# Attention: prompt pairs from slot 0 of the first period, blocks in the order 2, 3, 0, 1

## What is computed

```python
def fox_prompt_attention(q, k, v, cum, valid):   # 4 blocks of 128 queries, 16 heads of 64
    s = jnp.einsum('bqhd,bkhd->bhqk', qi, k).astype(jnp.float32) * FOX_SCALE
    s = s + jnp.swapaxes(ci, 1, 2)[..., :, None] - cum_k[:, :, None, :]
    p = jax.nn.softmax(jnp.where(mask, s, MASK_VALUE), axis=-1)
    return jnp.einsum('bhqk,bkhd->bqhd', p.astype(v.dtype), v)
...
k_past = cache_k[page_table].reshape(DB, P, FOX_HEADS, FOX_DH)
v_past = cache_v[page_table].reshape(DB, P, FOX_HEADS, FOX_DH)
o = fox_sample_attention(q, k_past, v_past, cum_past, k_new, v_new, cum_new)
```

## Time and profile before

| | us |
|---|---|
| median of 3 runs | 2024.12 |
| lowest, highest | 2014.05, 2030.99 |
| the profiled execution | 2018.67 |
| its span, first to last instruction | 2016.5 |
| PE busy in the span | 1935.1 |
| DVE, ACT, POOL busy | 1040.9, 691.8, 440.3 |
| mean granted clock | 0.984 |

### The profile page before, as it was taken

How to read it: one execution, slowest core, us unless ns; L and a number is a source line. 1 busy time by engine, 2 the same in 40 slices (tenths; PEclk the granted TensorE clock), 3 DMA queues, 4 the chain that set the end, 5 groups by cost and what they waited for, 6 DMA issues and landing times.

```text
span 2016.5 us, 35645 instructions
## 1 busy us (share of the span) xinstructions
PE 1935.1 (96%) x14855; PEld 1779.8 (88%) x14855; DVE 1040.9 (52%) x1170; ACT 691.8 (34%) x898; POOL 440.3 (22%) x106
## 2 busy tenths in 40 slices
PE   6999999999899999999999999799998999999998
PEld 6979969979789999999999999655555999999998
DVE  4445245245446865455532535567664566646461
ACT  4131232232224325152531432244444332515251
POOL 2302402412303312121133233000001332121212
PEclk9999999999999999999999999899998999999999
DMA  5351441441243223222232221789996222222231
GB/s 162 126 165 45 137 164 46 137 157 52 95 167 95 84 68 101 82 85 83 98 94 64 65 84 44 215 233 279 280 277 222 85 84 78 90 84 96 71 104 47
DMA packets 197349, 239.13 MB, mean 119 GB/s; under 512 B 16419, under 2 KB 168355, under 8 KB 197027
## 3 DMA queue, kind: packets, MB, share of 16 engines
q1 hardware_dynamic: 175650, 183.27, 30.1%
q10 hardware_dynamic: 21488, 53.46, 8.1%
q0 software_dynamic: 80, 0.52, 0.1%
HBM read 210.77 MB, written 26.12 MB: 117 GB/s over the span
## 4 chain that ended last, share of the span: by engine, by line
PE 68%; issue 16%; DVE 6%; POOL 4%; ACT 2%; DMA 2%; SPq 1%; ACTq 1%; DVEq 0%; POOLq 0%
PE PS L800 12%; PE PS L801 11%; PE PS L802 11%; POOL w_lo L740 4%; PE PS L816 4%; PE PS L818 4%; PE PS L817 4%; PE PS L879 3%; PE PS L880 3%; PE PS L881 3%; PE PS L1349 2%; PE PS L1304 1%; PE PS L1250 1%; PE PS L1284 1%; DVE k_page_t L2366 1%
## 5 line engine op out<-in xcount | busy, mean ns | idle before, releaser
L740 POOL TENSOR_TENSOR w_lo<-w_raw,w_hi 128x2048 fp32r<-128x2048 f32 (+2 forms) x101 | 439.1, 4348 | 1543.5 <-ACT w_hi L1453 1543.5
L1453 ACT ACTIVATE w_hi<-w_raw 128x2048 fp32r<-128x2048 f32 (+2 forms) x101 | 178.1, 1764 | 644.4 <-PE PS L802 419.1
L800 PE MATMUL PS<-hidden_hi,w_hi 128*128 128x296 f32 (+1 forms) x1024 | 304.4, 297 | 0.7 <-DVE hidden_tmp L2135 0.6
L802 PE MATMUL PS<-hidden_hi,w_lo 128*128 128x296 f32 (+1 forms) x1024 | 304.7, 298 | 0.0
L801 PE MATMUL PS<-hidden_lo,w_hi 128*128 128x296 f32 (+1 forms) x1024 | 304.2, 297 | 0.0
L800 PE MATMUL PS<-x_hi,w_hi 128*128 128x296 f32 (+1 forms) x896 | 269.4, 301 | 5.4 <-DVE x_lo L1898 2.8
L801 PE MATMUL PS<-x_lo,w_hi 128*128 128x296 f32 (+1 forms) x896 | 268.4, 300 | 0.0
L802 PE MATMUL PS<-x_hi,w_lo 128*128 128x296 f32 (+1 forms) x896 | 267.8, 299 | 0.0
L879 PE MATMUL PS<-w_hi,x_hi 128*128 128x256 f32 x800 | 225.8, 282 | 0.4 <-DVE fox_gate L2287 0.4
L881 PE MATMUL PS<-w_lo,x_hi 128*128 128x256 f32 x800 | 224.8, 281 | 0.0
L880 PE MATMUL PS<-w_hi,x_lo 128*128 128x256 f32 x800 | 224.6, 281 | 0.0
(11 more groups left out here) (294 smaller groups left out, 3869.4 us busy)
## 6 DMA issues: line engine op xcount, KB each, us to landing
w_raw<-in_w_mlp_up SPq DMA_DIRECT2D x32, 1024.0 KB, 5.4
w_raw<-in_w_mlp_down SPq DMA_DIRECT2D x32, 1024.0 KB, 5.1
k_page<-in_cache_k SPq DMA_DIRECT2D x256, 128.0 KB, 5.7
v_page<-in_cache_v ACTq DMA_DIRECT2D x56, 512.0 KB, 8.0
w_raw<-in_w_ret_in SPq DMA_DIRECT2D x24, 1024.0 KB, 5.4
sample_state<-in_state_ret SPq DMA_DIRECT2D x32, 512.0 KB, 5.3
out_state_ret_sample<-sample_state ACTq DMA_DIRECT2D x32, 512.0 KB, 4.3
w_raw<-in_w_ret_out SPq DMA_DIRECT2D x16, 512.0 KB, 3.5
```

Of the source, the lines that this page charges most:

```text
L740: pool.tensor_tensor(lo, raw, hi.bitcast(F32), ALU.subtract).then_inc(lo_done, 1)
L800: pe.matmul(o, wh[:, w], xh[:, t, cols], start=(t == 0), stop=False)
L802: last = pe.matmul(o, wl[:, w], xh[:, t, cols], start=False, stop=(t == kt - 1))
L1453: act.activation(part(WH[n.slot], n, kt), part(WR[n.slot], n, kt), ACT.Copy).then_inc(hi_done, 1)
```

## The change

Pair j stands in slot 4b + i, two slots earlier in the program than before, and its block is (j + 2) % 4: the slots keep the blocks 2, 3, 0, 1, and the heads t advance with the period. So pairs 0 and 1 (blocks 2 and 3 of the first two heads) fill slots 0 and 1 of the first period, and slots 0 and 1 of the last period have no new pair. In the first period the key pages are turned in slots 1, 2, 2, 3 (two, four and two of them) instead of two in each slot. The waits follow the numbers, and `values(1)` has a place of its own in slot 2 of the first period. `normed_probs`, `probs_copy`, `probs_t`, `values`, `maximum` and `gated` take their block from `block_of(j)` in the same way as the two shown.

```diff
         def pair_at(b, i):
-            return 4 * b + i - 2
+            return 4 * b + i
+
+        def block_of(j):
+            return (j + 2) % 4
...
             def scores(j):
-                t, qb = j // 4, j % 4
+                t, qb = j // 4, block_of(j)
...
             def probs_t_s(b):
                     if half:
-                        pe.wait_ge(pv_evac, 4 * b + 3)
+                        pe.wait_ge(pv_evac, min(4 * b + 5, NPAIR))
...
             def slot0(b, j):
                 if live(j):
                     scores(j)
                 if b > 1:
                     out_t(b - 2)
-                if live(j):
+                if live(j - 1):
                     probs_t(j - 1)
                 if b > 0:
                     pair_scores(b - 1, 3)
                     new_scores(b - 1)
+                if live(j - 1):
+                    values(j - 1)
+
+            def slot1(b, j):
+                if live(j - 1):
+                    probs_t(j - 1)
                 if live(j):
-                    values(j - 1)
-
-            def slot1(b, j):
-                if live(j):
-                    probs_t(j - 1)
                     scores(j)
+                if live(j - 1):
                     values(j - 1)
                 if b < DB:
                     bias(b)
...
             def slot2(b, j):
...
                 if b > 0:
                     probs_copied(b - 1)
+                if live(j - 1):
                     probs_t(j - 1)
                 if b == 0:
+                    values(j - 1)
                     pair_scores(b, 0)
                 if b < DB:
                     pair_scores(b, 1)
...
             def slot3(b, j):
                 if live(j):
                     scores(j)
+                if live(j - 1):
                     probs_t(j - 1)
+                if b < DB:
                     pair_scores(b, 2)
...
             def exp(j, par):
-                n = keys_of(j % 4)
-                act.wait_ge(mx_done, 2 * j + (2 if j % 4 == 3 else par + 1))
+                n = keys_of(block_of(j))
+                act.wait_ge(mx_done, 2 * j + (2 if block_of(j) == 3 else par + 1))
...
+            FIRST_TURNS = ((), (0, 1), (2, 3, 4, 5), (6, 7))
             for b in range(DB + 1):
...
-                    if k:
+                    if k and b > 0:
                         turn_page(NPAGE * b + 2 * i)
...
-                    if k:
+                    if k and b > 0:
                         turn_page(NPAGE * b + 2 * i + 1)
+                    for p in FIRST_TURNS[i] if b == 0 else ():
+                        turn_page(p)
                     if i != 1 and live(j - 1):
                         gated(j - 1)
```

More of the change, by code:

```diff
@@ L1264, in probs_t @@
                     pe.wait_ge(pn_done, 2 * j + par + 1)
-                    for kb in range(j % 4 + 1):
-                        at = P * kb + (NKEY + NMETA if par else NKEY - keys_of(j % 4))
+                    for kb in range(block_of(j) + 1):
+                        at = P * kb + (NKEY + NMETA if par else NKEY - keys_of(block_of(j)))
                         last = pe.transpose(PS[:, 4 + 2 * par, P * kb:P * kb + P], PP[:, at:at + P], ident)
@@ L1800, in probs_copy @@
             def probs_copy(j):
-                m = P * (j % 4 + 1)
+                m = P * (block_of(j) + 1)
                 for par in range(2):
@@ L2343, in maximum @@
             def maximum(j, par):
-                n, m = keys_of(j % 4), P * (j % 4 + 1)
-                dve.wait_ge(s_ready, 2 * j + (2 if j % 4 == 3 else par + 1))
+                n, m = keys_of(block_of(j)), P * (block_of(j) + 1)
+                dve.wait_ge(s_ready, 2 * j + (2 if block_of(j) == 3 else par + 1))
                 own = score_cols(par, n)[:, m - P:m] if par == 0 else score_cols(par, n)[:, n - P:n]
```

## The result

The changed kernel took 2031.96 us in the median of 19 runs (2019.62 to 2040.05), the kernel before 2019.26 beside it (19 runs, 2013.69 to 2030.99). The ratio is 1.0041, 95% interval 1.0026 to 1.0056, so the change costs about 8 us, within 1%. The profiled execution of the changed kernel took 2028.98 us, span 2026.9, at a mean clock of 0.980 (before 2018.67, 2016.5 and 0.984).

The account below looks back on a forecast made before the run. PE's own work was taken to bound the middle periods, with waits at the two ends. Last period -5.8, first +10.4 and second +0.9 summed to +5.5 us on 2021.4: forecast 2027 us, range 2015 to 2038.

Parts of the forecast that it names:

- Base: Starting time of the forecast, set midway between the profiled 2018.67 and the three-run median 2024.12: 2021.4 us.
- Middle, 0: Six middle attention periods, 30.29 us each: slots keep their blocks and mix, so no change in time.
- Last period: End of the attention phase: two pairs fewer, 20.4 us against 26.22, -5.8 (-9.0 to -0.3).
- Sixteen matmuls (one page): Value pages of the last period: one page priced at 1.94 us at half level, 0.93 at full.
- Behind it: After the last period: gating, fox_y and the projection's weights hang on the pages' end and move with it.
- First period: Head of the attention phase: two added pairs, a 4.3 us PE gap and late pages, 30.6 us, +10.4.
- half level to its end: Upper bound of the first period: the half clock level holding throughout adds 4.4, to 35 us (+15).
- Second period: Second attention period: late page 8 adds 3.0 us, to 33.3, +0.9 because the earlier half level is gone.
- Rival (c): Both ends: half level or late pages hold longer, +10 to +12, 2032 us; chance 0.23.
- Rival (a): First period bound by PE's work, not the chain: it grows +2, kernel gains 3 to 4, 2018 us; chance 0.12.
- rival (b): Clock stays at full level at both ends: -0.7, 2021 us; chance 0.13 together with rival (d).
- rival (d): Pairs cost the same anywhere if pair 0's chain is as well covered: 0, 2021 us; chance 0.13 with rival (b).

Follow-up runs that it names:

- the two repeats: The changed kernel profiled again without any edit, twice: first periods 28.74 and 28.83 us; the second repeat's ratio to the kernel before was 1.0044.
- The five executions of that order: Profiles of the changed kernel, its repeats and two versions with only `o_tok`'s scaling altered: first period 34.1 us in two, 28.8 in three.
- e1_early_turns: Changed kernel with key pages 0 to 3 turned in slot 0 of the first period: ratio 1.0008 to the kernel before.
- e3_both: Changed kernel with key pages 0 to 3 turned in slot 0 and two extra bias writes behind the first scores: ratio 0.9979 to the kernel before.
- e5_covered: Changed pair positions, with bias and a page product behind the first scores and pages turned earlier: 2013.46 us, ratio 0.9954 to the kernel before.
- e2_filled_gap: Changed kernel with sample 0's bias written twice more behind pair 0's scores, filling PE's gap: ratio 1.0034 to the kernel before.

## Why the prediction came out as it did

The forecast was 2027 us from a sum of +5.5; the measured ratio gives +8 and the median 2031.96. The sign and "within 1%" were right, and +8 lies in the forecast's own bracket of +3 to +9. That it came this near is partly luck: the second period cost about 5 us more than forecast and the end gained about 3.5 more, and the first period came near its forecast only as a mean of two lengths.

- **Base.** I set 2021.4; the median of the 19 runs of before is 2019.26.
- **Middle, 0.** Measured +0.95 with the same PE work. The period itself I had wrong: 181.72 / 6 = 30.29 holds one period of 32.91, and an undisturbed one is 29.76, before and after.
- **Last period, forecast -5.8 (20.4).** The value pages could start 9.05 us into it, where 9.2 was forecast, and the clock was mostly back (0.89). The failed step is "Sixteen matmuls (one page)": `x16` were two pages of eight rows each. The rows say so, x16 + x48 = 64 for eight pages. (In the program a page is four matmuls, `v_page_148` x4 in the order of instructions, and each stands twice in the trace.) All eight took 5.5 us, not 10.6, and the period 15.6, below my bound of 17.2. Against 26.22 that is -10.6.
- **Behind it, forecast nothing ("moves with it").** It cost +1.4 in the profiled execution, 0.9 and 0.8 in the two repeats. GpSimd's first split of the projection's weights now covers DVE's scaling, as the rows above show; in the earlier trace rows the scaling lasted 0.26. Last period and tail together: -9.3.
- **First period, forecast 30.6 (+10.4, bounds +7.4 to +15).** The gap was 4.59 for 4.3 and the first page turn stood 16.66 us into the period for 17.1 (1308.2 - 1291.1). The period was 34.08 and, in the repeats, 28.74 and 28.83. The five executions of that order average 30.9, but none is near it: the half level held for 22 us or let go early. My "half level to its end" bound of 35 is nearly the one case; the other lies between the forecast and the bound with the full level, 27.6.
- **Second period, forecast 33.3 (+0.9).** The chain was right almost to the end: DVE free for page 8 at 4.2 us into the period (forecast 4.3), page 8 turned from 7.3 (6.9), pair 3 gated from 11.1 (11.3). The wait itself, 3.08, was longer than the "1 to 2 us" among the signs, which my own times, 1328.6 - 1326, had at 2.6. The step that failed is its price, "3.0 us go into the period ... for the half level that cost it 8 us at twice the time before is gone". That half level was gone, the clock was 1.00 up to the gap. But the wait also held the inverse sums of pair 4, PE stood for 3.66 + 0.70 us, and a new half level followed for 17.09. Of the 39.64 - 29.76 = 9.9 us over an undisturbed period, 2.7 are more idle time (4.42 against 1.71) and 7.2 are longer work (PE busy 35.22 against 28.05). The mean of the five is 38.6, +6.3; e1_early_turns and e3_both, without the wait, still have 35.8, so about 3 us of it go with the wait and the rest with a half level that no run here traces to its cause.

With the means of five for the first two periods the sum is +10.8 + 6.3 - 9.3 = +7.8, near what the ratio shows. That is no proof of the split: before was profiled once, and the six middle periods of these five executions took 180.4 to 189.4 us. Rival (c), with its +10 to +12, is half met. The half level did hold nearly to the end of the first period, in two executions of five; its other condition, a landing at 6 us, was not seen, page 8 was there at 7.3 us for 6.9. The ratio lies between the forecast and (c), and the median, 2031.96, on (c)'s 2032, but on a base 2 us lower than the one I set. Rival (a) needed a first period of less than 26 and rival (b) the full clock; neither was seen. The condition of rival (d), a covered first chain, is what e5_covered brings, and there the change gains instead of costing nothing: the first two periods together cost 3.6 us more than before (26.80 + 29.27 against 52.50) and the end gives back more than that.

The rule of the Trainium skill that I weighed ("DMA: Bandwidth & Descriptors", Rules for kernel authors), to issue loads early, is borne out here: e3_both, with the early turns, has 0.9979 where e2_filled_gap has 1.0034, about 11 us of the whole time. That is more than the 3.0 us that I gave it; the rows of their second periods show 3.4 of it (39.20 and 35.81).

## What to carry to other kernels

Moving work to the head of a phase is paid for by what covered that head: see that its first chain has independent work beside it, and that whatever releases the loads still runs early. Look for work at the half level behind a gap on PE before you price a wait by its length; here a period with 2.7 us more idle time had 7.2 us more of PE work too. A short or filled gap was no safeguard against it. Divide a row's `x16` by units of work that you can count in the trace (64 rows for eight value pages) before turning it into a price; the source, with four matmuls a page, would have misled as well. And profile a kernel more than once before you explain a period: the same program gave 28.7 and 34.1 us.

## What the runs showed of the hardware that was not expected

- The half level held for 22.30 us with PE busy for 21.62 of them, at a DMA share of 0.32; in other executions of the same kernel the same 4.59 us gap was followed by a first period 5.3 us shorter.
- In e1_early_turns the clock fell to the half level for 13.66 us in a period with no more idle time on PE (1.60 us) than an undisturbed one (1.71).
- DVE's scaling of `o_tok`, from SBUF to SBUF, is held until a 4.5 us GpSimd operation that runs beside it ends, and ends 0.04 to 0.08 us after it: 0.74 to 4.23 us in eleven executions instead of 0.25, in both forms tried (with a factor per partition, and as a product of two tensors). A reduction (0.57 to 0.59), a reciprocal (0.16 to 0.17) and a product out of PSUM (0.42 to 0.48) beside the same split are not slowed.
